# Going by halves of 256 tokens from one layer to the next in a two-block transformer kernel on one NeuronCore

## The chip, the cores and the metric

The kernel runs on one core of a Trainium2 chip (trn2). The metric is the device time of one execution in microseconds (us). Engines are named as the profile names them: PE is TensorE (PEld its weight loads), DVE is VectorE, ACT is ScalarE, POOL is GpSimd, SP is SyncE, which issues the weight transfers.

## The reference: what is computed

There are 512 tokens of 2048 features, in f32. The first block has one layer, the second has two. Cut to what matters here:

```python
# first block
u = rmsnorm(h, g_pre);  z = u @ w_in          # attention and a gated scan make y from z
h = h + rmsnorm(y @ w_out, g_post)            # new residual 1
gate = sigmoid(h @ w_pg);  e = p @ w_pp
h = h + rmsnorm(gate * e, g_ple)              # new residual 2
# second block, two layers
for l in range(2):
    z = rms_norm(h, pre_norm_g[l]) @ w_in[l]  # retention, differential attention and an LRU make y
    h = h + rms_norm(y @ w_out[l], post_norm_g[l])   # new residual 3 behind layer 0, the output behind layer 1
```

Each new residual is the input of the next matrix product at once: `w_pg` behind residual 1, the layer's `w_in` behind residuals 2 and 3.

## The kernel before, in words

**Tiling.** Features lie on the 128 partitions, tokens along the row, so an activation is 16 feature tiles of 128 x 512. A weight tile (128 output features) is 16 blocks of 128 x 128 and gives one output tile of 128 x 512 in one PSUM bank. A product of f32 precision is made of three fp32r matmuls: operand and weight are split into a high part (rounded to fp32r) and a low part (the rest), and PE adds high x high, high x low and low x high. An output tile is 48 matmuls of 512 columns, in four quarters of four blocks (`quarter`, L315 on). All weight tiles are numbered in one row (T_OUT: `w_out` of the first block, T_PG: `w_pg`, T_L2: the two layers).

**Who does what for the weights.** SP loads tile t into one of two raw buffers as soon as POOL has made the low parts of tile t-2 (L229). ACT makes the high part of a quarter (`high`, L710), once the raw tile has landed and PE has used this quarter of the tile before (`w_free`). POOL subtracts it from the raw tile (L262). `high_apart` (L717) and `low_parts_apart` (L270) do the same into a separate buffer, `next_weights`, which holds two whole tiles and lets them be converted ahead.

**Who does what for a new residual.** The last 16 tiles of a product go to PSUM banks; ACT squares each and copies it, times the gain, to `mixed` (L947, L722), DVE adds the squares up (L1633), and PE sums over the partitions with a matmul by ones, last `sum_rows_last` (L382 and L384, for the sum so far and for tile 15). ACT makes the inverse root with Ln and Exp (L729, L731) into a PSUM bank, `turned`. Then `new_operand` on DVE goes through the 16 tiles, four alone and then by pairs: `scale_tiles` (L1653, mixed times root), `add_tiles` (L1658, into the residual in `work`), and `low_tile` (L1616; L1618 with the next norm's gain) for the tiles one step behind. Between the add and the low tile ACT makes the high copy in `operand` (L916, L918). PE starts the next product with `three_tiles` (L341): three output tiles side by side in three banks, 9 matmuls per operand tile, so that PE follows the operand tile by tile; two of the weight tiles are those in `next_weights`, the third is in the usual place. PE takes operand tile k when `u_ready` says that its low part is there.

At residual 2 the 16 tiles are the gate: ACT makes Exp (L1112), DVE adds one, takes the reciprocal and multiplies by e (L1264, L1266, L1829), ACT squares (L1116) and copies with the gain.

**Behind residuals 2 and 3** the next norm's sum is taken while PE is at the first tiles: ACT issues four transfers of the residual to `out` (L1154), squares its 16 tiles (L1158), with conversions of weights between, DVE adds them up (L1631, L1633), and PE takes the ones matmul (L377) in the middle of the tile that follows the next one, at its second quarter. At residual 1 ACT issues four loads of e into `mixed` (L1103) between the high copies instead.

**Order.** Each engine's order is written out by hand in this file; there is no planner. An engine runs its instructions in order, so an instruction that waits holds back everything behind it on its engine. In `out_slots` ACT's order at the end is: tile 14, the eight conversions into `next_weights`, square and copy of tile 15, the high part of quarter 0 of the third weight tile, then Ln and Exp.

## Time and profile before

| | |
|---|---|
| Time, median of 3 runs | 3036.14 us (3035.97 to 3036.76) |
| The profiled execution's own time | 3036.43 us |
| Its span on the profile | 3034.6 us |
| PE busy | 2955.4 us (97%), 17162 matmuls |
| PEld busy | 2385.6 us (79%) |
| DVE busy | 1649.8 us (54%) |
| ACT busy | 1284.9 us (42%) |
| POOL busy | 1315.0 us (43%) |
| Mean granted clock of PE | 0.991 |

The times are what the device reports for an execution; the span runs from the first to the last profiled instruction; times in the rows are us from the span's start. A row of the page or of the grouped view ends with the busy time, the mean duration in ns and the idle time before, with what ended it. In the timeline a row has start and duration of an instruction, or of several like it that follow each other (x2); in square brackets stand the idle time of its engine before it and what ended that. Durations of matmuls overlap: what counts is how far apart they start.

### The profile page before, as it was taken

Reading aid. Unit: us, or ns where it says so; the run is one execution under the profiler, and the core shown is the slowest. Engines: PE = TensorE matmul, PEld = TensorE weight load, DVE = VectorE, ACT = ScalarE, POOL = GpSimd, SP = SyncE. Lnnn points to the kernel's source line nnn. Section 1 sums busy time; section 2 is a strip of 40 time slices with the busy share of each in tenths; the row PEclk is TensorE's granted clock in tenths of the full one; section 3 lists DMA queues with packets and bytes.
Section 4 is the critical chain, followed back from the end, with each engine's and each line's share of the span. In section 5 each row is a group of like instructions: output and inputs, shape, how many; then the busy total and the mean of one; then the engine's idle time right before and its main releaser. Section 6 shows DMA issues by size and latency. Waiting matters only on the chain.

```text
span 3034.6 us, 48369 instructions
## 1 busy us (share of the span) xinstructions
PE 2955.4 (97%) x17162; PEld 2385.6 (79%) x17162; DVE 1649.8 (54%) x2349; ACT 1284.9 (42%) x2468; POOL 1315.0 (43%) x1002
## 2 busy tenths in 40 slices
PE   8999999999999999989999999999999999999997
PEld 6888888877777787767887878788778878787886
DVE  5367666655656315657565664561275656654412
ACT  6545444354556333443333333453343333344432
POOL 4444444443433343553444444344444444444444
PEclk9999999999999999999999999999999999999999
DMA  6223222222222323233222222232242222222322
GB/s 238 102 90 111 83 83 76 77 84 83 78 77 80 125 97 139 90 118 125 105 87 91 87 85 82 83 142 100 104 156 88 95 87 96 84 84 80 143 97 97
DMA packets 60880, 305.72 MB, mean 101 GB/s; under 512 B 5712, under 2 KB 6096, under 8 KB 29776
## 3 DMA queue, kind: packets, MB, share of 16 engines
q1 hardware_dynamic: 38224, 259.54, 24.0%
q10 hardware_dynamic: 22528, 44.50, 4.2%
q8 instruction: 77, 1.26, 0.2%
q14 instruction: 51, 0.42, 0.0%
HBM read 285.67 MB, written 18.35 MB: 100 GB/s over the span
## 4 chain that ended last, share of the span: by engine, by line
issue 56%; POOL 32%; PE 9%; POOLq 1%; DMA 1%; ACT 1%; DVE 0%; DVEq 0%; ACTq 0%; SPq 0%
POOL w_low L262 31%; PE z L325 8%; DMA w_raw<-in_wt 1%; POOLq L261 1%; POOL next_weights L270 0%; PE scores L325 0%; PE v_bank L358 0%; PE z L358 0%; ACT u_high L722 0%; DVE mixed L1647 0%; POOLq L296 0%; DVE work L1266 0%; POOLq L284 0%; POOLq L129 0%; ACT w_high L710 0%
## 5 line engine op out<-in xcount | busy, mean ns | idle before, releaser
L262 POOL TENSOR_TENSOR w_low<-w_raw,w_high 128x512 fp32r<-128x512 f32 x932 | 1254.3, 1350 | 1700.0 <-ACT w_high L710 1692.5
L325 PE MATMUL z<-u_high,w_high 128*128 128x512 f32 x3408 | 1347.6, 395 | 2.6 <-POOL w_low L262 1.8
L325 PE MATMUL z<-u_high,w_low 128*128 128x512 f32 x3408 | 1328.4, 390 | 0.0
L325 PE MATMUL z<-u_low,w_high 128*128 128x512 f32 x3408 | 1327.0, 389 | 0.0
L710 ACT ACTIVATE w_high<-w_raw 128x512 fp32r<-128x512 f32 x928 | 578.7, 628 | 1223.0 <-PE z L325 1128.3
L325 PEld LDWEIGHTS z<-u_high,w_high 128*128 128x128 f32 x3408 | 640.1, 188 | 160.2 <-issue 23.3
L325 PEld LDWEIGHTS z<-u_high,w_low 128*128 128x128 f32 x3408 | 639.6, 188 | 136.1
L325 PEld LDWEIGHTS z<-u_low,w_high 128*128 128x128 f32 x3408 | 640.5, 188 | 127.1
L1633 DVE TENSOR_TENSOR work<-work 128x512 f32<-128x512 f32 x87 | 99.9, 1148 | 365.0 <-ACT work L947 351.7
L1260 DVE TENSOR_TENSOR work<-z,work 128x512 f32<-128x512 f32 x110 | 76.1, 692 | 122.7 <-PE z L325 101.8
L1292 DVE SCALAR_TENSOR_TENSOR work<-z,work 32x512 f32<-32x512 f32 (+1 forms) x176 | 120.9, 687 | 2.4
L735 ACT ACTIVATE work<-work 128x512 f32<-128x512 f32 x72 | 45.4, 631 | 145.4 <-DVE work L1272 92.1
L341 PE MATMUL z<-u_high,next_weights 128*128 128x512 f32 x192 | 72.1, 417 | 21.1 <-DVE u_low L1618 13.6
L722 ACT ACTIVATE values_spread<-work 32x512 f32<-32x512 f32 x128 | 80.6, 630 | 19.4 <-DVE work L1449 16.4
L1316 DVE TENSOR_TENSOR work<-o_bank,head_norm 128x512 f32<-128x512 f32 x28 | 19.4, 692 | 112.5 <-ACT head_norm L748 112.5
L1279 DVE TENSOR_TENSOR mixed<-work 128x512 f32<-128x512 f32 (+1 forms) x35 | 24.3, 694 | 85.4 <-ACT work L739 85.4
L1288 DVE SCALAR_TENSOR_TENSOR work<-z,work 128x512 f32<-128x512 f32 x56 | 38.7, 692 | 58.7 <-PE z L325 56.7
L1296 DVE TENSOR_TENSOR work<-work 128x512 f32<-128x512 f32 x56 | 65.4, 1168 | 5.2
L341 PEld LDWEIGHTS z<-u_high,next_weights 128*128 128x128 f32 x192 | 38.5, 200 | 35.5 <-issue 23.4
L1347 DVE TENSOR_TENSOR work<-work 128x512 f32<-128x512 f32 x56 | 55.0, 983 | 18.8 <-ACT work L722 10.8
L722 ACT ACTIVATE work<-work 128x512 f32<-128x512 f32 (+1 forms) x96 | 58.3, 639 | 13.9 <-DVE work L1347 9.7
L1474 DVE SCALAR_TENSOR_TENSOR work<-work 128x512 f32<-128x512 f32 x72 | 60.8, 845 | 6.0 <-issue 0.9
(281 smaller groups left out, 3243.7 us busy)
## 6 DMA issues: line engine op xcount, KB each, us to landing
w_raw<-in_wt SPq DMA_DIRECT2D x241, 1024.0 KB, 4.8
out_hT<-work ACTq DMA_DIRECT2D x8, 1024.0 KB, 8.7
work<-out_hT ACTq DMA_DIRECT2D x8, 1024.0 KB, 10.4
work<-in_xT SPq DMA_DIRECT2D x4, 1024.0 KB, 17.2
e_scratch<-work ACTq DMA_DIRECT2D x1, 4096.0 KB, 16.7
work<-in_xT ACTq DMA_DIRECT2D x4, 1024.0 KB, 10.9
work<-in_dec ACTq DMA_DIRECT2D x12, 256.0 KB, 2.7
work<-rope_tables ACTq DMA_DIRECT2D x10, 256.0 KB, 2.8
```

The source lines that it names most:

```text
L262: pool.tensor_tensor(WL[:, 4 * q:4 * q + 4, :], RAW[:, t.odd, 512 * q:512 * q + 512].rearrange("p (k c) -> p k c", k=4), WH[:, 4 * q:4 * q ...
L325: mm = pe.matmul(bank[:], w[:, k, :], u[:, k, :], start=(k == 0 and n == 0), stop=(k == KT - 1 and n == 2))
L341: mm = pe.matmul(bank[:], w[x], u[:, k, :], start=(k == 0 and n == 0), stop=(k == KT - 1 and n == 2))
L710: act.activation(WH[:, 4 * q:4 * q + 4, :], RAW[:, n.odd, 512 * q:512 * q + 512].rearrange("p (k c) -> p k c", k=4), ACT.Copy).then_inc(se ...
L722: i = act.activation(dst, src, ACT.Copy, **kw)
L735: act.activation(row(r), row(r), ACT.Exp, scale=-1.0)
L1260: v.tensor_tensor(dst, (Z[t.odd] if bank is None else bank)[:], row(RSTD), ALU.mult).then_inc(sem("z_free"), 1)
L1292: i = v.scalar_tensor_tensor(out=row(TM)[o:o + half], in0=z[x:x + half, :], scalar=-scale if first else scale, in1=row(sin)[o:o + half], o ...
L1296: v.tensor_tensor(row(dst), row(dst), row(TM), ALU.add)
L1347: i = v.tensor_tensor(x, x, y, ALU.mult)
L1474: v.scalar_tensor_tensor(out=R_, in0=R_, scalar=-1.0 / f, in1=TB, op0=ALU.add, op1=ALU.mult)
L1633: i = v.tensor_tensor(row(ACC), row(ACC), row(SQ0 + s), ALU.add)
```

## The change

At the three new residuals (behind `w_out` of the first block, behind `w_pg`, behind `w_out` of layer 0) everything from the last output tile to the three opening tiles goes in two halves of 256 tokens:

- PE: tile 15 is `split_tile`: all 48 matmuls for tokens 0 to 255 into one bank, then all 48 for tokens 256 to 511 into another, each with 256 columns. The ones matmuls are two halves too: `sum_first_half` within the second half of tile 15 (behind its first quarter, at residual 2 behind its third), `sum_second_half` within the first half of the opening tiles (behind operand tile 1, at residual 2 behind tile 4). `three_tiles` goes through the 16 operand tiles twice, 144 matmuls of 256 columns each time. Quarters of weights are given back in the second pass only.
- ACT: square and copy of tile 15, Ln and Exp by halves (`root_half`, in a bank for each half). `operand` makes 16 high copies of 128 x 256, then 16 more. The three other conversions of the third weight tile stand behind the copies 0, 3 and 5 of the first half at all three residuals (before: at residuals 1 and 3 among the copies, at residual 2 ahead of the root). What tile 15's second half needs of ACT stands among the copies too.
- DVE: `new_operand` runs twice, tile 0 and 1 alone and then seven pairs, with 256 elements of each tile; at residual 2 the second half's gate stands behind its third step.

The rest of the kernel, the four loads of e, the four transfers to `out` and the chain of squares are as before; the loads of e stand behind the copies 7, 11, 13 and 15 of the second half.

The diff, cut (PE, then ACT, then DVE):

```diff
@@ -214,6 +214,8 @@
             return (XW if buf is None else buf)[:, r, :].rearrange("p (k c) -> p k c", k=4)
         PH, PL = UL[:, 12:14, :], UL[:, 14:16, :]
         ROOT = TP[1]
+        SPLIT_BANK, SUM_BANK, ROOTS = [TP[0], VB], SC[1], [TP[1], SC[1]]
+        HALVES = [slice(0, S // 2), slice(S // 2, S)]
         OUT_BANK = SC[0]
         FIRST = {1: [Z[0], Z[1]], 2: [Z[0], VB]}
         LAST = [SC[0], SC[1], TP[0], OB, Z[0], Z[1]]
...
-                    mm.then_inc(sem("w_free"), 3)
+            def three_tiles(t, gen, g, n, at):
+
+                pe.wait_ge(sem("z_free"), t.times(1, -T_HGG - 1))
+                for half, cols in enumerate(HALVES):
+                    for q in range(4):
+                        if half == 0:
+                            pe.wait_ge(sem("l_ready"), t.times(4, 8 + q + 1))
+                        for k in range(4 * q, 4 * q + 4):
+                            if half == 0:
+                                pe.wait_ge(sem("u_half"), g * 16 + k + 1)
+                            else:
+                                pe.wait_ge(sem("u_ready"), gen * 16 + k + 1)
+                            c = slice((k - 4 * q) * P, (k - 4 * q + 1) * P)
+                            hi = [XW[:, r + q, c] for r in XHI] + [WH[:, k, :]]
+                            lo = [XW[:, r + q, c] for r in XLO] + [WL[:, k, :]]
+                            for x, bank in enumerate((Z[0], Z[1], SC[0])):
+                                for i, (w, u) in enumerate(((hi, UH), (hi, UL), (lo, UH))):
+                                    mm = pe.matmul(bank[:, cols], w[x], u[:, k, cols], start=(k == 0 and i == 0),
+                                                   stop=(k == KT - 1 and i == 2))
+                            if half == 0 and k == at:
+                                sum_second_half(n)
+                        if half == 1:
+                            mm.then_inc(sem("w_free"), 3)
+
+            def split_tile(t, n, g, at):
+
+                pe.wait_ge(sem("z_free"), t.times(1, -1 - T_HGG))
+                for half, cols in enumerate(HALVES):
+                    for q in range(4):
+                        if half == 0:
+                            pe.wait_ge(sem("l_ready"), t.times(4, q + 1))
+                        for k in range(4 * q, 4 * q + 4):
+                            for i, (w, u) in enumerate(((WH, UH), (WH, UL), (WL, UH))):
+                                mm = pe.matmul(SPLIT_BANK[half][:, cols], w[:, k, :], u[:, k, cols], start=(k == 0 and i == 0),
+                                               stop=(k == KT - 1 and i == 2))
+                        if half == 1:
+                            mm.then_inc(sem("w_free"), 1)
+                            if q == at:
+                                sum_first_half(n, g)
+                    if half == 0:
+                        mm.then_inc(sem("z_half"), 1)
+
+            def sum_first_half(n, g):
+
+                c = HALVES[0]
+                pe.wait_ge(sem("sq_used"), PRIMED + n + 15)
+                pe.matmul(SUM_BANK[:, c], ONES[:], row(ACC)[:, c], start=True, stop=False)
+                pe.wait_ge(sem("sq_half"), g + 1)
+                pe.matmul(SUM_BANK[:, c], ONES[:], row(SQ1)[:, c], start=False, stop=True).then_inc(sem("sum_half"), 1)
+
+            def sum_second_half(n):
+
+                c = HALVES[1]
+                pe.matmul(OB[:, c], ONES[:], row(ACC)[:, c], start=True, stop=False)
+                pe.wait_ge(sem("sq_ready"), n + 16)
+                pe.matmul(OB[:, c], ONES[:], row(SQ1)[:, c], start=False, stop=True).then_inc(sem("sq_used"), 1)
 
             def pair_step(t, k, gen, block=1):
 
...
-            three_tiles(Tile(T_PG), 2)
+            for q in range(4):
+                quarter(Tile(T_OUT + 14), q)
+            split_tile(Tile(T_OUT + 15), 16, 0, 0)
+            three_tiles(Tile(T_PG), 2, 0, 16, 1)
             for m in range(3, 6):
...
                 for s in range(2):
                     for q in range(4):
                         quarter(Tile(T_PG + s, (2, i)), q)
-            sum_rows_last(32)
+            for q in range(4):
+                quarter(Tile(T_PG + 14), q)
+            split_tile(Tile(T_PG + 15), 32, 1, 2)
 
             for l in range(LAYERS):
-                three_tiles(Tile(T_L2 + l * PER_LAYER), l * 2 + 3)
+                three_tiles(Tile(T_L2 + l * PER_LAYER), l * 2 + 3, l + 1, 64 if l else 32, 1 if l else 4)
                 for m in range(3, LRU_TILES):
                     for q in range(4):
                         quarter(Tile(T_L2 + R_LX + m, (PER_LAYER, l)), q, None, LX_BANK[m])
...
+            def root_half(half, wait, done):
+
+                c = HALVES[half]
+                act.wait_ge(*wait)
+                act.activation(row(ACC)[:, c], (OB if half else SUM_BANK)[:, c], ACT.Ln, bias=CS[:, C_EPS:C_EPS + 1], scale=1.0 / D)
+                act.drain()
+                act.activation(ROOTS[half][:, c], row(ACC)[:, c], ACT.Exp, scale=-0.5).then_inc(sem(done), 1)
+
+            def operand(t, g, new, second, scale=None, done=None):
+
+
+
+                n = t.times(4)
+                steps = {0: lambda: high(t.plus(1), 1, n - 2), 3: lambda: high(t.plus(1), 2, n - 1), 5: lambda: high(t.plus(1), 3, n)}
+                for half, cols in enumerate(HALVES):
+                    for m in range(KT):
+                        if half:
+                            act.wait_ge(sem("h_new"), m + 1 + new)
+                        else:
+                            act.wait_ge(sem("h_half"), g * 16 + m + 1)
+                        act.activation(UH[:, m, cols], W[:, H + m, cols], ACT.Copy,
+                                       scale=1.0 if scale is None else scale[:, m:m + 1]).then_inc(sem("uh_ready" if half else "uh_half"), 1)
+                        if half == 0 and m in steps:
+                            steps[m]()
+                        if half == 0 and m in second:
+                            second[m]()
+                        if half and m in (7, 11, 13, 15):
+                            q = (7, 11, 13, 15).index(m)
+                            if done is not None:
+                                done(q, *((0, 8), (8, 12), (12, 14), (14, 16))[q])
+                            if q < 3:
+                                high(t.plus(2), q, n + 3 + 3 * q)
...
                             high_apart(t.plus(16 + x), q, x)
-                one(t.plus(15), 15, 1, n + 14, quarters=0)
                 if last == "three":
+                    a = HALVES[0]
+                    act.wait_ge(sem("z_half"), split + 1)
+                    act.wait_ge(sem("sq_used"), PRIMED + n + 14)
+                    act.activation(row(SQ1)[:, a], SPLIT_BANK[0][:, a], ACT.Square).then_inc(sem("sq_half"), 1)
+                    copy(MIX[:, 15, a], SPLIT_BANK[0][:, a], scale=gain[:, 15:16])
                     high(t.plus(17), 0, t.times(4, 61))
-                inv_root(OB, row(ACC), D, (sem("sq_used"), PRIMED + n + 16), root, ROOT[:])
+                    root_half(0, (sem("sum_half"), split + 1), "root_half")
+                else:
+                    one(t.plus(15), 15, 1, n + 14, quarters=0)
+                    inv_root(OB, row(ACC), D, (sem("sq_used"), PRIMED + n + 16), root, ROOT[:])
...
@@ -1139,16 +1213,36 @@
             pg_square(14, 0, 15)
             for q in range(4):
                 high_apart(Tile(T_L2 + 1), q, 1)
-            pg_evict(Tile(T_PG + 15), 1, 32 + 14)
-            for q in range(4):
-                high(Tile(T_L2 + 1), q, 4 * T_L2 - 3 + q)
-            pg_square(15, 1, 16)
-            inv_root(OB, row(ACC), D, (sem("sq_used"), PRIMED + 48), "root_ready", ROOT[:])
+            def pg_evict_half(half, wait, done):
+
+                c = HALVES[half]
+                act.wait_ge(*wait)
+                act.activation(row(SQ1)[:, c], SPLIT_BANK[half][:, c], ACT.Exp, scale=-1.0).then_inc(sem(done), 1)
+
+            def pg_square_half(half, wait, done):
+
+                c = HALVES[half]
+                act.wait_ge(*wait)
+                act.activation(row(SQ1)[:, c], MIX[:, 15, c], ACT.Square).then_inc(sem(done), 1)
+                act.drain()
+                copy(MIX[:, 15, c], MIX[:, 15, c], scale=PR1[:, G_PLE + 15:G_PLE + 16])
+
+            act.wait_ge(sem("sq_used"), PRIMED + 32 + 14)
+            pg_evict_half(0, (sem("z_half"), 2), "ze_half")
+            high(Tile(T_L2 + 1), 0, 4 * T_L2 - 3)
+            pg_square_half(0, (sem("pg_half"), 1), "sq_half")
+            root_half(0, (sem("sum_half"), 2), "root_half")
 
             for l in range(LAYERS):
                 three = 4 * (T_L2 + l * PER_LAYER)
-                operand(Tile(T_L2, (PER_LAYER, l)), W[:, H:H + 16, :], PR2[:, l, G2_PRE:G2_PRE + 16], l * 16 + 16,
-                        weights=False, taken=three + 3, third=three if l else None)
+                if l:
+                    second = {2: lambda: out_second(Tile(T_L2 + R_OUT), 64, PR2[:, 0, G2_POST:G2_POST + 16]),
+                              4: lambda: root_half(1, (sem("sq_used"), PRIMED + 80), "root_ready")}
+                else:
+                    second = {1: lambda: pg_evict_half(1, (sem("w_free"), 4 * T_L2), "z_free"),
+                              4: lambda: pg_square_half(1, (sem("pg_prod"), 16), "sq_ready"),
+                              6: lambda: root_half(1, (sem("sq_used"), PRIMED + 48), "root_ready")}
+                operand(Tile(T_L2 + l * PER_LAYER), l + 1, l * 16 + 16, second, PR2[:, l, G2_PRE:G2_PRE + 16])
                 act.wait_ge(sem("h_new"), l * 16 + 32)
                 for g in range(4):
                     act.dma_start(out[4 * g:4 * g + 4].rearrange("m p t -> p m t"), W[:, H + 4 * g:H + 4 * g + 4, :]
...
@@ -1658,20 +1752,44 @@
                 v.tensor_tensor(W[:, H + m:H + m + k, :], W[:, H + m:H + m + k, :], MIX[:, m:m + k, :],
                                 ALU.add).then_inc(sem("h_new"), k)
 
-            def new_operand(root, n, loaded, scale=None):
-
-                wait_apart("root_ready", root)
+            def new_operand(root, n, g, loaded, scale=None, between={}):
+
+                wait_apart("root_half", g + 1)
                 v.wait_ge(sem("x0_loaded"), 16)
                 v.wait_ge(sem("h_loaded"), loaded)
-                lows = 0
-                for m, k in ((0, 1), (1, 1), (2, 1), (3, 1), (4, 2), (6, 2), (8, 2), (10, 2), (12, 2), (14, 2)):
-                    scale_tiles(m, k)
-                    add_tiles(m, k)
-                    while lows < m:
-                        low_tile(lows, n, W[:, H:H + 16, :], scale)
-                        lows += 1
-                for m in range(lows, 16):
-                    low_tile(m, n, W[:, H:H + 16, :], scale)
+                for half, cols in enumerate(HALVES):
+                    if half:
+                        wait_apart("root_ready", root)
+                    lows = 0
+                    for m, k in ((0, 1), (1, 1), (2, 2), (4, 2), (6, 2), (8, 2), (10, 2), (12, 2), (14, 2)):
+                        b = ROOTS[half][:, cols]
+                        b = bass.AP(b.tensor, b.offset, [b.ap[0], [0, k], [1, S // 2]])
+                        v.tensor_tensor(MIX[:, m:m + k, cols], MIX[:, m:m + k, cols], b, ALU.mult)
+                        v.drain()
+                        x = W[:, H + m:H + m + k, cols]
+                        v.tensor_tensor(x, x, MIX[:, m:m + k, cols], ALU.add).then_inc(sem("h_new" if half else "h_half"), k)
+                        while lows < m:
+                            low_half(lows, n, g, half, scale)
+                            lows += 1
+                        if half == 0 and m in between:
+                            between[m]()
+                    for m in range(lows, KT):
+                        low_half(m, n, g, half, scale)
...
@@ -1850,10 +1968,22 @@
                         pg_sum(s, i * 2 + 32 + s + 1)
             pg_tile(14, 0, T_PG + 13)
             pg_sum(0, 47)
-            pg_tile(15, 1, T_PG + 14)
+            def pg_last_half(half, wait, done):
+
+                c = HALVES[half]
+                v.wait_ge(*wait)
+                s = row(SQ1)[:, c]
+                v.tensor_scalar(s, s, 1.0, None, ALU.add)
+                v.drain()
+                v.reciprocal(s, s)
+                v.drain()
+                v.tensor_tensor(MIX[:, 15, c], s, MIX[:, 15, c], ALU.mult).then_inc(sem(done), 1)
+
+            pg_last_half(0, (sem("ze_half"), 1), "pg_half")
 
             for l in range(LAYERS):
-                new_operand(l + 2, l * 32 + 48, l * 64 + 64, PR2[:, l, G2_PRE:G2_PRE + 16])
+                new_operand(l + 2, l * 32 + 48, l + 1, l * 64 + 64, PR2[:, l, G2_PRE:G2_PRE + 16],
+                            {} if l else {2: lambda: pg_last_half(1, (sem("z_free"), T_PG + 16 - T_HGG), "pg_prod")})
 
                 sum_squares(l * 32 + 48)
                 wait_apart("rstd_ready", l + 2)
```

## Rows read from the trace of the kernel before

A line of "..." stands for rows left out.

**Rows 1.** Page, part 1: busy time, share of the span and instructions.

```profile
PE 2955.4 (97%) x17162; PEld 2385.6 (79%) x17162; DVE 1649.8 (54%) x2349; ACT 1284.9 (42%) x2468; POOL 1315.0 (43%) x1002
```

**Rows 2.** Waits of PE: waiting line, releaser: us in total, times, longest.

```profile
PE z L341 <- DVE u_low L1618: 13.6, 5, 5.6
PE o_bank L377 <- DVE work L1633: 1.6, 2, 0.8
```

**Rows 3.** Timeline of PE, residual 1.

```profile
1160.78 1.02 PE L382 MATMUL o_bank<-work,ones 128*128 128x512 f32 x2
...
1168.43 0.77 PE L341 MATMUL z<-u_high,next_weights 128*128 128x512 f32 x1 [5.68 <-DVE u_low L1616]
...
1205.88 0.39 PE L341 MATMUL scores<-u_high,w_low 128*128 128x512 f32 x1
1206.11 0.39 PE L325 MATMUL scores<-u_high,w_high 128*128 128x512 f32 x1
```

**Rows 4.** Windows, residual 1: stretch, then PE, PEld, DVE, ACT, POOL busy, clock.

```profile
1168.40:1173.60 5.20, 5.17 (x12) 4.13 (x13) 5.05 (x7) 1.83 (x4) 1.75 (x1) 0.50 0.00 0
```

**Rows 5.** Timeline of ACT, residual 1.

```profile
1157.14 2.19 ACT L717 ACTIVATE next_weights<-w_raw 128x512 fp32r<-128x512 f32 x4 [3.21 <-DMA w_raw<-in_wt]
...
1162.90 0.63 ACT L710 ACTIVATE w_high<-w_raw 128x512 fp32r<-128x512 f32 x1 [0.75 <-DMA w_raw<-in_wt]
```

**Rows 6.** Timeline of POOL, residual 1.

```profile
1152.45 5.15 POOL L270 TENSOR_TENSOR next_weights<-w_raw,next_weights 128x512 fp32r<-128x512 f32 x4 [0.29 <-ACT next_weights L717]
...
1169.05 1.75 POOL L262 TENSOR_TENSOR w_low<-w_raw,w_high 128x512 fp32r<-128x512 f32 x1 [4.18 <-ACT w_high L710]
```

**Rows 7.** Timeline of DVE, residual 1.

```profile
1164.87 0.69 DVE L1653 TENSOR_TENSOR mixed<-mixed,turned 128x512 f32<-128x512 f32 x1 [12.16 <-ACT turned L731]
...
1169.57 1.78 DVE L1616 TENSOR_TENSOR u_low<-work,u_high 128x512 fp32r<-128x512 f32 x1
...
1173.23 1.21 DVE L1653 TENSOR_TENSOR mixed<-mixed,turned 128x1024 f32<-128x1024 f32 x1
1174.52 1.23 DVE L1658 TENSOR_TENSOR work<-work,mixed 128x1024 f32<-128x1024 f32 x1
...
1179.40 1.28 DVE L1616 TENSOR_TENSOR u_low<-work,u_high 128x512 fp32r<-128x512 f32 x2
...
1199.39 1.96 DVE L1616 TENSOR_TENSOR u_low<-work,u_high 128x512 fp32r<-128x512 f32 x2 [1.47 <-ACT u_high L916]
```

**Rows 8.** Timeline of DVE, residual 2.

```profile
1352.09 3.35 DVE L1266 RECIPROCAL work<-work 128x512 f32<-128x512 f32 x1
...
1361.62 0.69 DVE L1653 TENSOR_TENSOR mixed<-mixed,turned 128x512 f32<-128x512 f32 x1 [4.27 <-ACT turned L731]
...
1379.45 1.41 DVE L1618 SCALAR_TENSOR_TENSOR u_low<-work,params,u_high 128x512 fp32r<-128x512 f32 x2
```

**Rows 9.** Timeline of ACT, residual 2.

```profile
1347.28 2.18 ACT L717 ACTIVATE next_weights<-w_raw 128x512 fp32r<-128x512 f32 x4
...
1394.20 0.71 ACT L918 ACTIVATE u_high<-work,params  x1
...
1397.54 1.76 ACT L1158 ACTIVATE work<-work 128x512 f32<-128x512 f32 x3 [2.63 <-issue]
...
1401.20 0.63 ACT L710 ACTIVATE w_high<-w_raw 128x512 fp32r<-128x512 f32 x1 [1.11 <-PE scores L341]
```

**Rows 10.** Timeline of PE at the ones matmul, residual 2.

```profile
1418.22 1.12 PE L377 MATMUL o_bank<-work,ones 128*128 128x512 f32 x2 [0.80 <-DVE work L1633]
```

**Rows 11.** The same, residual 3.

```profile
2247.51 1.13 PE L377 MATMUL o_bank<-work,ones 128*128 128x512 f32 x2 [0.81 <-DVE work L1633]
```

**Rows 12.** Timeline of PE, 128-column matmuls, and the page's weight loads.

```profile
1601.68 0.39 PE L533 MATMUL o_bank<-work 128*128 128x128 f32 x2
1601.91 0.39 PE L535 MATMUL o_bank<-work 128*128 128x128 f32 x2
...
L325 PEld LDWEIGHTS z<-u_high,w_high 128*128 128x128 f32 x3408 | 640.1, 188 | 160.2 <-issue 23.3
```

82 lines of the change are left out of this document (35 added, 47 removed).

## The prediction

> **What bounds the kernel now.** I read the page first: PE is busy for 97% of the span and DVE for 54% [rows 1], so only time in which PE stands can come back. The waits of PE, longest in total first, say where [rows 2]: at L341, the three opening tiles, PE waits for `u_low` of DVE (L1618 at the second and third residual; L1616 at the first is alike), and twice 0.8 us at L377, the ones matmul over the squares of the new residual. The timeline at the first new residual [rows 3]: tile 15 ends at 1160.78, two pairs of ones matmuls follow, and the first opening matmul starts at 1168.43 after 5.68 us of idle; the next tile starts at 1206.11. Matmuls start 0.2265 us apart, so the 144 of this stage need 32.6 us, and the stretch has 45.3. The windows show what follows the idle: 12 matmuls in 5.2 us at granted clock 0.50 (1.2 GHz, 0.427 us each) [rows 4]. The third residual is alike. The second is longer, because the sigmoid runs before its norm: a reciprocal alone is 3.35 us [rows 8].
>
> But the stage has a second limit. After the idle DVE works nearly without a gap from 1164.87 to 1201.35, 36.5 us [rows 7], against 32.6 of PE. **DVE is within a few us of being the bound of exactly these stages.** And the end of a second or third residual is set later still: ACT squares the residual, DVE adds, and PE stands 0.8 us at L377 until the last add is done [rows 2, 10, 11].
>
> **The change, part by part.** I call the residuals R1, R2, R3.
>
> *PE's own work.* Per residual 48 + 144 matmuls of 512 columns become 384 of 256. None of this size with changing weights is in the trace. From below, half of 0.2265 is 0.113. The f32 matmuls of L533 and L535 with 128 columns, each behind a weight load of its own, start 0.11 us apart (two in 0.23) [rows 12], so a load fits into that. From above stands the 0.188 us that a load is busy [rows 12]. I take 0.1165, near the first, since the row that overlaps loads is the nearest. An opening stage is then 288 x 0.1165 + 0.9 for the second half's ones matmuls = 34.5 us.
>
> *Start of the first half, R1.* Half A of tile 15 ends at 1160.78 - 5.4 = 1155.3. ACT is then in its queue at the four conversions of 1157.14, done at 1159.33; behind them square, copy, and the conversion of w_high of 1162.90, which waits for the weight transfer [rows 5]. That transfer can't be earlier: it needs the buffer that POOL gives back at 1152.45 + 5.15 = 1157.6 [rows 6], and nothing there moves. Ln and Exp stand behind this conversion, as before. So the square can be early, the root can't. Shorter Ln and Exp bring 0.5 us, of which POOL's conversion of 1163.6, now in DVE's way, takes a little: DVE starts 0.4 earlier, not 5. PE meanwhile waits inside tile 15 for the square (from 1157.2 to 1159.8, 2.6 us), ends at 1164.4, and gets its first operand near 1166.9 instead of 1168.43. R3 has the same rows and order, 0.4.
>
> *Start, R2.* ACT is free at 1347.28 + 2.18 = 1349.46 [rows 9]. Exp of half 0.4, plus one on DVE beside POOL 1.1, reciprocal 1.7 (half of 3.35) with its drains 0.2, product 0.7, square 0.5, ones matmul 0.6, Ln and Exp 0.9: 1355.5, where DVE began at 1361.62 [rows 8]: 6.1 earlier.
>
> *DVE's length, the main term.* From the rows [rows 7]: an add behind its scale starts 0.08 after the scale's end, so 0.76 apart at 512 elements and 1.29 at 1024, or 1.035 ns an element; an instruction without a drain starts 0.08 before the last one ends, so an add takes 0.61 or 1.14 and a low tile 0.60 (two in 1.28). With 256 elements: scale 0.49, add 0.345, low 0.34. Before: 4 x (0.76 + 0.61) + 6 x (1.29 + 1.14) + 16 x 0.60 = 29.7. After, in each half: 2 x (0.49 + 0.345) + 7 x (0.76 + 0.61) + 16 x 0.34 = 16.7, twice 33.4: **3.7 more**. R2 and R3 use the scaled low tile, 0.66 (two in 1.41) [rows 8] and 0.395 in half: 30.6 becomes 35.2, 4.6 more. Together 12.9 us. What DVE took above the 29.7 in R1, 6.8, I keep: 1.47 is a wait for ACT, and six conversions of POOL stop it for 0.9 each (1.78 instead of 0.68 while POOL runs 1.75) [rows 6, 7]; the same six lie in the new stage. The ends for an instruction of 256: half of a whole one (12.9 falls to 0), and the whole fixed part exposed each time (below). I take the extrapolation, since 512 and 1024 lie on one line.
>
> The Trainium skill, VectorE: DVE Perf Modes, the section on the errata, says that a small tile pays a fixed latency of its own, about 151 cycles at 0.96 GHz for a tensor_tensor of f32, and advises tiles of 512 elements or more: a rule against this change. There are 32 more instructions per residual (68 for 36); at 0.157 us each that would be an estimate of 5.0 per residual, 15 in all instead of 12.9, and a time near 3043.6. The rows show part of this cost overlapped.
>
> *R1, the sum.* DVE ends at 1201.35 + 3.7 - 0.4 = 1204.65. The last two low tiles come 0.34 apart and PE needs 1.05 for each: PE ends 1.9 later, 1206.5. Before, 1206.11 [rows 3]: **+0.4**. By PE alone it would be 1166.9 + 34.5 = 1201.4, so 5 us of PE slack hide its waits, its pace, and a lower clock if that comes.
>
> *R2.* DVE's end: -6.1 + 4.6, + 2.6 for the gate of the second half, which the change puts into DVE's queue behind the third tile (0.3 + 1.7 + 0.4 and drains; it ran in the idle before), + 2.7 for three conversions of the third tile's weights, which fell in the idle and now fall in DVE's loop (3 x 0.9) = +3.8. Then the squares: ACT starts them when the last high copy and four output transfers are issued (first square 1397.54) [rows 9]. The last copy (1394.20 to 1394.91) came 1.3 before DVE's end, since two whole low tiles followed; now it comes 0.3 before: +1.0. The chain of squares then waited 1.11 us for PE to leave the stage [rows 9], and about as long once more for the next tile's first quarter; coming later, it no longer waits: -2.3. PE at L377 starts at 1418.22 + 2.5: **+2.5** [rows 10]. PE reaches that point 72 matmuls, 16.3 us, after its stage's end and stands there.
>
> *R3.* -0.4 + 4.6 + 1.0 - 2.3 = **+2.9** on 2247.51 [rows 11].
>
> Sum +5.8. Smaller: in R1 the transfers of `e` are issued some 14 us later, in half B, and land near 1206, just before the gate wants them at 1208; I count nothing (0 to 2). The old low clock costs little to lose: DVE had the last word. I round down to +5 for conversions that share one wait. The profiled execution took 3036.43, the median is 3036.14: forecast **3041**.
>
> **The rivals.**
> *DVE keeps ahead (faster).* For it: the idle of 5.68 us at R1 is real [rows 3], and PE starts 1.5 to 8 earlier. Against: the 36.5 us of DVE. If a half instruction cost half a whole one, 12.9 goes: 3028. If PE alone set the end, R1 gives -4.8, R3 -5, R2 1357.8 + 34.5 against 1418.22 - 0.8 - 16.3 = 1401.1, -8.8: 3017.
> *The weight load bounds the matmul (slower).* At 0.188 an opening stage is 55 us; R1 would end at 1223.8, +17.7, three times +53: 3089. It decides from 0.134 on, where 288 matmuls use up the 5 us of slack. Against: the 0.111 [rows 12].
> *ACT holds the high copies back (slower).* In half A the second half's square, copy, Ln, Exp and three conversions stand among the 16 high copies; Ln waits for PE's ones matmul, and DVE's low tiles wait behind. Price 2 to 3 us at each residual: 3048. It decides once the wait at Ln passes the 1.4 us that a scale and add give.
> *Nothing moves:* the halves cancel and DVE's end stays, 3036.
>
> **How the numbers follow.** A measurement here can tell about 0.2%, 6 us, from no change: same is 3030.1 to 3042.2. Forecast 0.55 (its own range 3034 to 3047, 0.35 of it within 0.2%, 0.20 slower), DVE ahead 0.19 (0.18 faster), ACT 0.14, weight load 0.05, nothing 0.07. Faster 0.18, same 0.43, slower 0.39. The range leaves out the weight load and the far side of the first rival: 3027 to 3051.
>
> **What would show it.** Right: DVE from first scale to last low tile 40 us in R1 instead of 36.5, 256-element instructions at 0.42, the root of half A at R1 starting near 1163.5 behind the conversion, PE idle in many pieces before `u_low` at the opening matmuls, and a longer wait at L377's ones matmul. Wrong: opening matmuls back to back (DVE ahead), starts 0.19 apart (load), or DVE waiting for `u_high` (ACT). The forecast falls if the root of half A comes before 1160, or if no wait at the sum of squares grows.

## The result, and the profile after

The changed kernel takes **3046.77 us** (median of 7 runs, 3044.88 to 3049.72), beside 3036.26 for the kernel before: ratio 1.0034, 95% interval 1.0023 to 1.0045, or 10.5 us slower. Its executions lie within 4.8 us of each other, those of before within 2.0. The profiled execution took 3046.97 us, its span is 3045.2 us and the granted clock 0.991. Half A is tokens 0 to 255, half B the rest.

The page's busy line [rows 1] and the waits of PE [rows 2] (waiting line, releaser, us in total, times, longest):

```profile
PE 2969.9 (98%) x17750; PEld 2423.9 (80%) x17750; DVE 1660.0 (55%) x2448; ACT 1295.6 (43%) x2529; POOL 1314.8 (43%) x1002
```

```profile
PE z L348 <- DVE u_low L1791: 9.8, 11, 2.2
...
PE o_bank L420 <- DVE work L1727: 6.5, 2, 4.0
...
PE scores L379 <- ACT work L1226: 4.0, 1, 4.0
PE scores L379 <- ACT work L1028: 3.9, 2, 2.0
...
PE z L348 <- DVE u_low L1789: 2.1, 4, 0.7
```

L348 is the opening stage (L341 before): its waits fell from 21.1 us (13.6 behind L1618, 7.5 behind L1616), in pieces of up to 5.7, to 11.9 in fifteen smaller ones. L379 is new: the wait inside tile 15. **L420 is the ones matmul over the squares (L377 before), and its waits rose from 1.6 to 6.5.**

R1 in the timelines of ACT, DVE and PE [rows 3, 5, 7]:

```profile
1156.93 2.19 ACT L771 ACTIVATE next_weights<-w_raw 128x512 fp32r<-128x512 f32 x4 [3.24 <-DMA w_raw<-in_wt]
1159.03 0.36 ACT L1028 ACTIVATE work<-turned 128x256 f32<-128x256 f32 x1
1159.29 0.46 ACT L776 ACTIVATE mixed<-turned,params 128x256 f32<-128x256 f32 x1
1162.65 0.63 ACT L764 ACTIVATE w_high<-w_raw 128x512 fp32r<-128x512 f32 x1 [2.90 <-DMA w_raw<-in_wt]
1163.19 0.46 ACT L960 ACTIVATE work<-scores,constants 128x256 f32<-128x256 f32 x1
```

```profile
1164.19 0.42 DVE L1767 TENSOR_TENSOR mixed<-mixed,turned 128x256 f32<-128x256 f32 x1 [11.72 <-ACT turned L962]
...
1201.15 1.64 DVE L1789 TENSOR_TENSOR u_low<-work,u_high 128x256 fp32r<-128x256 f32 x2 [1.17 <-ACT u_high L976]
```

```profile
1166.42 0.36 PE L348 MATMUL z<-u_high,next_weights 128*128 128x256 f32 x1 [0.48 <-DVE u_low L1789]
...
1204.66 0.28 PE L348 MATMUL scores<-u_high,w_low 128*128 128x256 f32 x1
1204.78 0.40 PE L327 MATMUL scores<-u_high,w_high 128*128 128x512 f32 x1
```

The root of half A (L960) stands behind the conversion that waits 2.90 us for the weights. DVE works 38.6 us, from 1164.19 to 1202.79, where it took 36.5. Matmuls of 256 columns start 0.12 us apart. The next tile begins 1.3 us earlier than before.

Now the ends of R2 and R3: ACT's first squares [rows 9], PE at the ones matmul [rows 10, 11], and windows of 3.4 us behind it (stretch, busy time of PE, PEld, DVE, ACT, POOL, then the granted clock):

```profile
1399.58 1.76 ACT L1252 ACTIVATE work<-work 128x512 f32<-128x512 f32 x3 [2.25 <-issue]
```

```profile
1416.62 0.39 PE L327 MATMUL turned<-u_high,w_low 128*128 128x512 f32 x1
1420.97 2.08 PE L420 MATMUL o_bank<-work,ones 128*128 128x512 f32 x2 [3.97 <-DVE work L1727]
...
2256.01 1.22 PE L420 MATMUL o_bank<-work,ones 128*128 128x512 f32 x1 [2.52 <-DVE work L1727]
```

```profile
1420.97:1424.40 3.43, 3.43 (x6) 2.11 (x7) 0.00 (x0) 0.26 (x1) 2.31 (x2) 0.50 0.90 289
1424.40:1427.80 3.40, 3.40 (x12) 2.66 (x12) 0.00 (x0) 0.20 (x1) 0.00 (x0) 0.68 0.29 118
...
2256.00:2259.40 3.40, 3.39 (x6) 2.08 (x7) 0.00 (x0) 0.00 (x0) 2.30 (x2) 0.50 0.93 298
2259.40:2262.80 3.40, 3.40 (x16) 2.79 (x16) 0.00 (x0) 1.19 (x2) 0.48 (x1) 1.00 0.26 108
```

In the kernel before, where PE stood only 0.8 us, the same stretch has 13 matmuls at full clock:

```profile
1418.22:1421.60 3.38, 3.38 (x13) 2.46 (x14) 0.00 (x0) 0.00 (x0) 2.33 (x2) 1.00 0.91 311
```

So PE stands 4.0 and 2.5 us, and **then runs at 1.2 GHz for a while**: a cost that no term of the forecast held.

The wait at R2 is 1.4 us longer than at R3, and ACT's squares do not explain it. From the first square to the ones matmul it takes 21.4 us at R2 and 20.0 at R3. DVE's adds are the same, but its idle time between them, for which the profile shows no releaser ("issue"), is 5.3 us in all at R2 and 3.7 at R3 (timeline of DVE, two rows of R2, then two of R3):

```profile
1408.25 0.69 DVE L1727 TENSOR_TENSOR work<-work 128x512 f32<-128x512 f32 x1 [0.57 <-issue]
1409.21 0.69 DVE L1727 TENSOR_TENSOR work<-work 128x512 f32<-128x512 f32 x1 [0.27 <-issue]
...
2243.60 0.69 DVE L1727 TENSOR_TENSOR work<-work 128x512 f32<-128x512 f32 x1 [0.45 <-issue]
2244.45 0.69 DVE L1727 TENSOR_TENSOR work<-work 128x512 f32<-128x512 f32 x1 [0.16 <-issue]
```

In the traces of the runs below the long gaps stand at R2 whenever DVE's instructions are those of the change (five more traces), and the short ones in the two that split R2 and edit DVE's instructions (more work for DVE, groups of four): there PE stands 2.5 us at R2 too. R3 always has the short ones. Why is not shown.

Counted from the start of tile 15 of each residual (1149.91, 1339.11, 2173.59 before; 1149.66, 1337.78, 2179.07 after):

| us from tile 15's start | before | after | difference |
|---|---|---|---|
| R1, next tile | 56.2 | 55.1 | -1.1 |
| R2, next tile / ones matmul | 61.8 / 79.1 | 62.7 / 83.2 | +0.9 / +4.1 |
| R2's ones matmul to R3's tile 15 | 755.4 | 758.1 | +2.7 |
| R3, next tile / ones matmul | 56.6 / 73.9 | 57.9 / 76.9 | +1.3 / +3.0 |
| R3's ones matmul to the end | 787.1 | 789.2 | +2.1 |

With the 0.25 by which R1's tile 15 starts earlier this is 10.6, the difference of the spans. In the third and fifth row the code is as before, and what differs is above all the clock behind the ones matmul. It is 0.50 for some 5.6 us at R2 and 3.4 at R3, and half of such a stretch is lost: 2.8 and 1.7 us. The other 0.4 of the fifth row is less than what traces at full clock differ by there (over 1 us).

### The profile page after: what moved, and what is told of

It reads as the page before. It is cut to its first block, busy times and chain, and to the rows that moved or that the text cites. A ratio compares the mean times of both kernels' runs of the same rounds, so it can differ in the third digit from the quotient of the medians.

```text
span 3045.2 us, 49473 instructions
## 1 busy us (share of the span) xinstructions
PE 2969.9 (98%) x17750; PEld 2423.9 (80%) x17750; DVE 1660.0 (55%) x2448; ACT 1295.6 (43%) x2529; POOL 1314.8 (43%) x1002
## 4 chain that ended last, share of the span: by engine, by line
issue 56%; POOL 32%; PE 9%; POOLq 1%; DMA 1%; ACT 1%; DVE 0%; DVEq 0%; ACTq 0%; SPq 0%
POOL w_low L264 31%; PE z L327 8%; DMA w_raw<-in_wt 1%; POOLq L263 1%; POOL next_weights L272 0%; PE scores L327 0%; PE v_bank L401 0%; PE z L401 0%; ACT u_high L776 0%; DVE mixed L1741 0%; POOLq L298 0%; DVE work L1360 0%; POOLq L286 0%; POOLq L129 0%; ACT w_high L764 0%
## 5 line engine op out<-in xcount | busy, mean ns | idle before, releaser
L327 PE MATMUL z<-u_high,w_high 128*128 128x512 f32 x3360 | 1329.2, 396 | 2.5 <-POOL w_low L264 1.8
L327 PE MATMUL z<-u_high,w_low 128*128 128x512 f32 x3360 | 1310.0, 390 | 0.0
L327 PE MATMUL z<-u_low,w_high 128*128 128x512 f32 x3360 | 1308.5, 389 | 0.0
L764 ACT ACTIVATE w_high<-w_raw 128x512 fp32r<-128x512 f32 x928 | 579.0, 628 | 1223.8 <-PE z L327 1127.4
L327 PEld LDWEIGHTS z<-u_high,w_high 128*128 128x128 f32 x3360 | 631.0, 188 | 157.8 <-issue 23.3
L327 PEld LDWEIGHTS z<-u_high,w_low 128*128 128x128 f32 x3360 | 630.6, 188 | 134.4
L327 PEld LDWEIGHTS z<-u_low,w_high 128*128 128x128 f32 x3360 | 631.4, 188 | 125.9
L348 PE MATMUL z<-u_high,next_weights 128*128 128x256 f32 x384 | 89.4, 295 | 12.0 <-DVE u_low L1791 9.8
L348 PEld LDWEIGHTS z<-u_high,next_weights 128*128 128x128 f32 x384 | 67.8, 195 | 16.2 <-DVE u_low L1791 8.8
```

The source lines that it names most:

```text
L327: mm = pe.matmul(bank[:], w[:, k, :], u[:, k, :], start=(k == 0 and n == 0), stop=(k == KT - 1 and n == 2))
L348: mm = pe.matmul(bank[:, cols], w[x], u[:, k, cols], start=(k == 0 and i == 0), stop=(k == KT - 1 and i == 2))
L764: act.activation(WH[:, 4 * q:4 * q + 4, :], RAW[:, n.odd, 512 * q:512 * q + 512].rearrange("p (k c) -> p k c", k=4), ACT.Copy).then_inc(se ...
```

## The experiments

Each was timed in five rounds beside the kernel before (medians 3036.2 to 3036.3). "The change" is the changed kernel; a median stands with its number of runs and the ratio's interval.

### Where the loss lies: the ones matmul

**The ones matmul later, in the change.** ACT's root over it moves as far.

```
-                        if m == 4 and q == 1:
+                        if m == 4 and q == 3:
                             sum_rows(row(ACC), OB, (sem("sq_used"), PRIMED + l * 32 + 64), "ss_done")
...
-                        if m == 4 and q == 2:
+                        if m == 5 and q == 0:
                             inv_root(OB, row(RSTD), D, (sem("ss_done"), l + 2), "rstd_ready")
```

> The changed kernel with the ones matmul over the squares of the new residual (R2 and R3) two quarters of a tile later in PE's order (5.4 us of matmuls), and ACT's root behind it two quarters later too. Theory (DVE and the chain of squares are late by 3 to 4 us, PE stands for them at this one matmul, 4.14 and 2.69 us, and runs behind it at half the clock for 6.8 and 3.4 us of records, some 5.1 us lost): both waits and both low clocks go, 6.8 + 5.1 = 11.9 us, 3035. Rival A (the wait is only the place where a late stage shows; banks and root are then late downstream): PE stands elsewhere before the first retention tile, 3044 to 3047. Rival B (the extra time lies in the opening stages, in the narrow matmuls): no change at all, 3047, with the two waits gone from the trace all the same.

Measured 3036.45 (11 runs, 0.9991 to 1.0009): 10.3 of the 10.5 us are back. PE no longer stands there (timeline of PE):

```profile
1425.16 1.02 PE L420 MATMUL o_bank<-work,ones 128*128 128x512 f32 x2
```

Both rivals fall: the wait comes back nowhere, and the opening stages, untouched, were not where most of the time went.

**The same move in the kernel before.**

> The kernel before with the same move of the ones matmul and of the root. Theory: only its two waits of 0.8 us are there to win and no clock falls behind them: 3034.5, same within 0.1%. If the move itself costs something downstream (root 5.4 us later), it shows here undisturbed: 3038 or more.

Measured 3034.52 (11 runs, 0.9986 to 1.0004), 1.7 below its neighbour, as expected: the two waits of 0.8, and no cost of the move, though the interval does not exclude a difference of nothing. So the 10.3 is not a gain that any kernel would have had: 8.6 of it belong to the change. With the wait out of the way in both, the halves are still 1.9 us slower (3036.45 against 3034.52); the intervals overlap, so it isn't shown that these are more than noise.

**The ones matmul earlier, in the kernel before** (q == 0, ACT's root at q == 1). Nothing is split here.

> The kernel before with the ones matmul one quarter (2.72 us) earlier, so that PE stands 3.5 us at it at R2 and at R3, as in the changed kernel, with nothing split. Theory: 5.4 us of waits, and behind each the granted clock falls for 3.4 to 6.8 us of records (1.7 to 3.4 lost): 3045 to 3048, nearly the whole loss of the change. Rival C (the low clock of the changed kernel comes from its many small idle pieces in the opening stage, not from this wait): clock stays at full, 3041.6. Rival A (downstream slack absorbs a wait here): 3036 to 3038.

Measured 3045.71 (7 runs, 1.0019 to 1.0041), +9.5. Timeline and windows:

```profile
1419.10 1.63 PE L377 MATMUL o_bank<-work,ones 128*128 128x512 f32 x2 [3.49 <-DVE work L1633]
```

```profile
1419.60:1423.00 3.40, 3.40 (x8) 2.35 (x7) 0.00 (x0) 0.00 (x0) 0.57 (x1) 0.50 0.90 335
1423.00:1427.00 4.00, 4.00 (x19) 3.25 (x18) 0.23 (x1) 1.84 (x3) 1.30 (x1) 1.00 0.07 23
...
2253.00:2256.40 3.40, 3.40 (x8) 1.99 (x8) 0.00 (x0) 0.00 (x0) 0.60 (x1) 0.58 0.93 337
```

Waits of 3.5 us were made by hand twice, 5.4 us more than before, and the clock fell behind both. Counted to the next tile 15 and to the end, less the quarter that now stands behind the ones matmul, the low clock costs 1.4 and 1.6 us. About 1 of the 9.3 by which this trace's span is longer lies ahead of R1, where nothing is changed. So two waits alone make some 8.4 us, most of the loss of the change, without any of its halves.

### Which residual carries it

**R2 put back to whole tiles** (its `split_tile`, `three_tiles`, `operand`, `new_operand` replaced by those of before).

> The changed kernel with R2 (the second residual) put back to whole tiles, R1 and R3 by halves. Theory: R2 carries 4.1 us of later ones matmul and 3.4 us of low clock: 3039 to 3040, no low clock behind its ones matmul. If R3 carried the loss: 3045.

Measured 3038.62 (11 runs, 0.9998 to 1.0016). PE stands 0.8 us at R2's ones matmul, as before the change; at R3 it stands 2.5, and in this trace the clock stays full behind it.

**R2 and R3 put back**, only R1 by halves.

> The changed kernel with R2 and R3 put back to whole tiles, only R1 by halves. Theory: R1 alone moves its next tile 1.1 us earlier against its own start, there is no ones matmul behind it, and nothing else differs: 3035.0, same as before within 0.1%; then R3 carries the difference to the run with only R2 whole (3038.6), 3.6 us. Rival (the narrow matmuls or the late transfers of e cost at R1 too): 3037 to 3038.

Measured 3034.85 (11 runs, 0.9986 to 1.0004). The steps against the kernel before (3036.31) are R1 -1.5, R3 +3.8, R2 +8.2: in sum 10.5. R2 is the costly one, as expected. R1's -1.5 is not clear of noise: its interval includes no change, and in its trace R1's next tile comes 56.4 us after the start of tile 15, where it was 56.2.

### What makes the chain late

**More work for DVE** in half B.

```
+                        if half:
+                            v.tensor_tensor(MIX[:, m, cols], MIX[:, m, cols], MIX[:, m, cols], ALU.max)
+                            v.drain()
                         v.tensor_tensor(MIX[:, m:m + k, cols], MIX[:, m:m + k, cols], b, ALU.mult)
```

> The changed kernel with one more DVE instruction of 256 elements (0.42 us and a drain, 0.5 in all, its result unused) ahead of each of the nine scales of half B, at R1, R2 and R3. Theory (DVE sets the end of the stage and of the chain of squares): the last low tile comes 4.5 us later each time, the next tile too, the wait at the ones matmul stays as it is since both shift: 3 x 4.5 = 13.5, 3060. Rival (PE with its narrow matmuls, or ACT, sets the end and DVE has room): 3047 to 3050.

Measured 3053.57 (5 runs, 1.0043 to 1.0070): +6.8, half of the 13.5. Each added instruction does take 0.50 us of DVE (timeline):

```profile
1184.37 0.42 DVE L1768 TENSOR_TENSOR mixed<-mixed 128x256 f32<-128x256 f32 x1
1184.87 0.69 DVE L1770 TENSOR_TENSOR mixed<-mixed,scores 128x512 f32<-128x512 f32 x1
```

DVE's stage grew by 3.1 us in R1, 5.9 in R2 and 2.1 in R3 instead of 4.5 each. In R1 its last wait for `u_high` shrank from 1.17 to 0.66, and POOL's conversions fell on other instructions; in R2 a wait of 3.0 for `u_high` came on top. PE's next point (the next tile of R1, the ones matmuls of R2 and R3) came 9 us later in all. I had also expected the waits at the ones matmul to stay. R2's fell from 3.97 to 2.56, with the short gaps of DVE described above, and PE went on at full clock, which returned 2.6 us. So the missing 6.7 us are in part an added instruction that shows only half to two thirds at R1 and R3, in part that clock. DVE's length sets the end; the rival (room on DVE) is out.

**Groups of four**, 12 DVE instructions fewer.

```
-                    for m, k in ((0, 1), (1, 1), (2, 2), (4, 2), (6, 2), (8, 2), (10, 2), (12, 2), (14, 2)):
+                    for m, k in ((0, 1), (1, 1), (2, 2), (4, 4), (8, 4), (12, 4)):
```

> The changed kernel with DVE's scales and adds of the later tiles in groups of four (1024 elements) instead of two: 12 instructions fewer per residual, the elements the same. Theory (DVE's fixed part per instruction is what the halves cost): 12 x 0.08 us (the part that stays visible between instructions without a drain) is 1 us per residual, up to 1.9 if the whole fixed part counts; the wait at the ones matmul falls from 4.1 and 2.7 to about 3.2 and 1.8, 3044, and 3042 if the low clock of R3 goes with it. Rival (ACT and PE wait for the coarser groups: the first tile of a group comes 0.5 to 0.7 us later): 3047 or slower, with more DVE waits for u_high.

Measured 3046.54 (5 runs, 1.0022 to 1.0050): no gain, near the rival's number. DVE's waits for `u_high` went from 4.9 us in all to 14.1; the longest is in R2 (timelines of ACT and DVE):

```profile
1373.40 0.47 ACT L960 ACTIVATE work<-o_bank,constants 128x256 f32<-128x256 f32 x1 [4.44 <-PE o_bank L386]
```

```profile
1374.80 0.48 DVE L1791 SCALAR_TENSOR_TENSOR u_low<-work,params,u_high 128x256 fp32r<-128x256 f32 x1 [3.16 <-ACT u_high L976]
```

ACT stands at the Ln of half B for PE's ones matmuls, and DVE behind it. In the change's own trace the same row waits 2.15 us:

```profile
1367.95 0.47 ACT L960 ACTIVATE work<-o_bank,constants 128x256 f32<-128x256 f32 x1 [2.15 <-PE o_bank L386]
```

The difference is how long PE runs at half clock in R2's opening: one window of the run with groups of four, then one of the change.

```profile
1366.00:1369.00 3.00, 2.34 (x11) 2.34 (x12) 2.93 (x5) 2.64 (x6) 0.35 (x1) 0.50 0.00 0
```

```profile
1366.00:1369.00 3.00, 3.00 (x23) 2.80 (x23) 2.75 (x4) 0.98 (x3) 0.78 (x1) 1.00 0.32 68
```

The total hides a gain elsewhere: in this trace the ones matmul of R2 waits 2.55 us and PE goes on at full clock, so that 2.5 us less are lost behind it, while R1's next tile comes 1.9 later and R2's ones matmul 0.8.

**The root of half B later on ACT**, here at R3; at R1 it is 4 and at R2 6 that become 10.

```
-                              4: lambda: root_half(1, (sem("sq_used"), PRIMED + 80), "root_ready")}
+                              10: lambda: root_half(1, (sem("sq_used"), PRIMED + 80), "root_ready")}
```

> The changed kernel with ACT's Ln and Exp of half B behind the eleventh high copy of half A instead of the fifth (R1, R3) or seventh (R2). Theory (the slower rival of the prediction is at work beside the main cause: Ln waits for PE's pair of ones matmuls, 2.1 us in the profile, up to 4.4 where PE's low clock of R2 lasts longer, and DVE's low tiles wait behind): DVE's waits for u_high of 1.1 to 2.8 us go, the executions spread less, 3044 to 3045. Rival (DVE's own work covers it): 3047 and the same spread.

Measured 3044.29 (8 runs, 1.0016 to 1.0037), 2.5 below the change, and the runs lie within 2.6 us instead of 4.8. In R2 ACT no longer waits at it:

```profile
1371.33 0.45 ACT L960 ACTIVATE work<-o_bank,constants 128x256 f32<-128x256 f32 x1
```

The forecast's third rival is real, and worth at most some 2.5 us in all: the intervals of the two overlap, and 1.2 us of it in the trace is a shorter stretch of low clock behind R2's ones matmul, where PE stood 3.98 us as in the change.

**The output transfers later**: the four issues leave the front of the squares and stand behind the squares of tiles 8, 10, 12 and 14.

> The changed kernel with the four output transfers of R2 and R3 issued on ACT among the last squares instead of ahead of the first. Theory (ACT's queue, 2.6 us of issues behind the last u_high copy, delays the chain of squares): the first square comes 1 to 2 us earlier, right behind the last low tile; the waits at the ones matmul fall to 2.5 and 1, the low clock of R3 and perhaps of R2 goes: 3038 to 3042. Rival (DVE's last low tile releases the chain anyway, and issues among the squares stretch it): 3046 to 3048.

Measured 3039.14 (11 runs, 1.0001 to 1.0019), 7.6 below the change. ACT squares right behind its last copy, DVE's adds begin where its last low tile ends (1.7 us behind it in the change), PE's waits fall to 1.29 and 0.80, and the clock stays (timelines of ACT and PE, window):

```profile
1399.91 0.89 ACT L976 ACTIVATE u_high<-work,params 128x256 fp32r<-128x256 f32 x2
1400.71 1.14 ACT L1249 ACTIVATE work<-work 128x512 f32<-128x512 f32 x2
```

```profile
1421.79 1.13 PE L420 MATMUL o_bank<-work,ones 128*128 128x512 f32 x2 [1.29 <-DVE work L1728]
...
2250.54 0.70 PE L420 MATMUL o_bank<-work,ones 128*128 128x512 f32 x1 [0.80 <-DVE work L1728]
```

```profile
1421.79:1425.20 3.41, 3.41 (x13) 2.53 (x14) 0.00 (x0) 1.09 (x2) 2.53 (x2) 1.00 1.03 336
```

### What held the split back at its start

**The root of half A ahead of the waiting conversion** (R1, R3).

```
-                    high(t.plus(17), 0, t.times(4, 61))
                     root_half(0, (sem("sum_half"), split + 1), "root_half")
+                    high(t.plus(17), 0, t.times(4, 61))
```

> The changed kernel with ACT's Ln and Exp of half A ahead of the conversion of w_high that waits 2.9 us for a weight transfer, at R1 and R3. Theory (that conversion holds the root, so the split of tile 15 brings nothing there): DVE starts 2.5 to 2.8 us earlier at R1 and R3 and ends as much earlier, the next tile of R1 comes 2 earlier, the wait at R3's ones matmul shrinks from 2.7 to below 1 and its low clock (1.7) goes: 3041. Rival (PE then stands for w_low of the same tile, and DVE for u_high): 3045 to 3047.

Measured 3043.57 (6 runs, 1.0018 to 1.0042), 3.2 below the change; 3041 was expected. The six lie 9.6 us apart (3041.77 to 3051.34), so the 3.2 is not clear of noise. The root starts 2.6 us earlier, and so does DVE:

```profile
1160.58 0.47 ACT L960 ACTIVATE work<-scores,constants 128x256 f32<-128x256 f32 x1 [0.91 <-PE scores L379]
...
1161.91 0.63 ACT L764 ACTIVATE w_high<-w_raw 128x512 fp32r<-128x512 f32 x1 [0.40 <-DMA w_raw<-in_wt]
```

```profile
1161.60 0.42 DVE L1767 TENSOR_TENSOR mixed<-mixed,turned 128x256 f32<-128x256 f32 x1 [9.48 <-ACT turned L962]
```

But DVE's loop in R1 is 1.7 longer: POOL's conversions now meet its first low tile (1.52 us instead of 0.42) and two of its four small adds, which take 647 ns on average instead of 426 (groups of DVE in R1's stretch, this run, then the run with R2 whole, whose R1 is as in the change).

```profile
L1770 DVE TENSOR_TENSOR work<-work,mixed 128x256 f32<-128x256 f32 x4 | 2.6, 647 | 0.3
```

```profile
L1832 DVE TENSOR_TENSOR work<-work,mixed 128x256 f32<-128x256 f32 x4 | 1.7, 426 | 0.3
```

I had also expected R3's wait at the ones matmul to shrink, and its low clock to go with it. The wait could not: PE's arrival and the chain of squares move together with DVE's end, and it is 2.55. The clock stayed full behind it all the same, which is 1.6 us of the gain of this trace. That can't be put down to the edit: behind the same wait the clock fell in the change.

### Put together

**Late ones matmul, early root of half A, late root of half B**; then the same with R2 whole.

> The changed kernel with three things put together: the ones matmul two quarters later, the root of half A ahead of the conversion that waits for the weights (R1, R3), the root of half B behind the eleventh high copy. Theory: from 3036.5 with the first alone, -3.2 for the second and about -2 for the third: 3031.3, 0.16% below the kernel before. If the gains overlap: 3033 to 3036.

> As the run before, with R2 put back to whole tiles. Theory: 3038.6 with R2 whole, less 3.3 at the ones matmuls, less 3.2 for the earlier roots of half A, less up to 1 for the root of half B: 3031 to 3032. If R2 by halves is now worth something (with the root of half B out of the way), this one is the slower of the two by 1 to 2 us.

Measured 3034.36 (11 runs, 0.9985 to 1.0003) and 3034.11 (11 runs, 0.9986 to 1.0004): the gains overlap, as the second half of the first expectation had it; the second missed its 3031 to 3032. Whether R2 goes by halves or whole makes no difference (0.25 us). In the trace of the first the earlier root lets DVE start 2.9 us earlier at R1 by tile 15's start, but its loop takes 41.7 us instead of 38.6, and PE's next tile comes no earlier. With these orders the split costs nothing, but neither run can be told from the kernel before, nor from the kernel before with the late ones matmul (3034.52). No version here is shown to beat it.

## Why the prediction was right or wrong

The forecast, 3041 with slower at 0.39 beside same at 0.43, put "same" slightly ahead, and slower by over 0.2% is what came. The measured 3046.77 lies in the range (to 3051), 5.8 above the forecast. That is in part luck: the range reached so far up for the rival of ACT (3048), and the largest part of the miss is a cost that the forecast had nowhere. Differences below are counted from the start of tile 15.

- **What bounds the kernel: right.** DVE was the second limit behind PE's idle. PE was given its operand 2 us earlier at R1 and 7 at R2, and the stages still ended where DVE ended. The first rival (DVE keeps ahead) is excluded by its own sign: PE waits in fifteen pieces.
- **PE's own work: right.** Matmuls of 256 columns start 0.12 apart (0.1165 taken), weight loads of 195 ns hidden beside them. The rival at 0.188 is out. (By the terms it gives, 1166.9 + 55, it would have ended R1 at 1221.9 rather than 1223.8.)
- **Start, R1 and R3: right.** The root came at 1163.19 (forecast near 1163.5), behind the conversion; the earlier root in the experiment shows that nothing else held it for the last 2.6 us.
- **Start, R2: right within 1 us.** 1354.70 with tile 15 starting 1.3 earlier than before, so 1356.0 on the forecast's clock; forecast 1355.5.
- **DVE's length, the main term: right in kind, too large in R1.** 38.6 us against 40, because three of POOL's conversions meet an add of half A and cost 0.35 each, not 0.9; the three that meet low tiles of half B cost 0.9 to 1.1. At R2 it took 43.9 (44.5 by the forecast's terms) and at R3 41.6 (41.7). By the Trainium skill, VectorE: DVE Perf Modes, the section on the errata, each of many small tiles pays its fixed latency. The rows bear that out in part only: instructions of 256 elements take 0.42 and start 0.34 apart in a row, and nine added ones of 0.50 lengthened the loops of R1 and R3 by 3.1 and 2.1. The estimate that went with it, 3043.6 (3043.1 if 2.1 is added to the forecast's 3041), came nearer to the result, but DVE's stages were no longer than the forecast's own terms; the loss behind them brought it there.
- **R1, the sum +0.4: measured -1.1.** That shorter loop: what POOL's conversions cost DVE was taken over from before at its old price. The late loads of `e` cost nothing, as counted: they are issued 1.2 to 8.8 us later, not 14, and DVE never waits for them.
- **R2, the sum +2.5: measured +4.1.** DVE's end came 3.7 later, forecast 3.8. Two terms behind it failed, in opposite directions.
  - **"Coming later, it no longer waits: -2.3" was mis-sized.** The chain's two waits for PE (1.11 and 1.04) did go, but from the first square to the ones matmul it took 21.4 us where it had taken 20.7, +0.7. DVE's adds and the gaps between them set its pace, not ACT; 1.4 us of it are the longer gaps. With the short ones it would have been -0.7, still not -2.3.
  - **"Now it comes 0.3 before: +1.0" was wrong.** The last high copy ended at 1397.33, 1.25 before DVE's end where it had been 1.35, since both last low tiles still follow it. The first square came 3.4 later, where 4.8 was forecast.
- **R3, the sum +2.9: measured +3.0, but by luck.** DVE's end came 4.0 later (4.2), the first square 3.6 (5.2), and the chain took 0.6 less (2.3 less): the same two errors, which cancel here.
- **The missing term: the clock behind the longer wait, 4.8 us in the table, some 4.5 of it by the low stretches.** The forecast wrote that slack hides "a lower clock if that comes", and looked for it only in the opening stage. Behind the ones matmul PE has no slack. The parts add up: -0.25 and -1.1 at R1, +4.1, +2.7, +3.0 and +2.1 are the 10.6.
- **The third rival (ACT holds the high copies back) was not exclusive.** It acts beside the main cause; its price, 2 to 3 per residual, is at most 2.5 for all three.

What stays open: why the low clock in R2's opening lasts longer in some traces. It does so in kernels whose code is the same up to there (DVE's stage of R2 takes 43.9 us in the change, 46.2 with the late output transfers), and the spread shrinks once ACT's Ln no longer depends on PE's progress; I did not vary it by itself. Open too is what makes DVE's gaps between the adds of R2 long or short.

## What to carry to other kernels

Before splitting work to start the next stage earlier, find what sets that stage's end: an engine that works without a gap through it gets only more instructions from the split. Price a wait of PE outside the stages with slack as the wait plus what the clock may lose behind it, and look there first for a remedy: moving one matmul by 5.4 us of its own queue brought the time 10.3 of 10.5 us down (1.7 of them it gives without the change too), where four remedies ahead of it brought between 0.2 and 7.6. And compare traces wait by wait before a gain is put down to an edit: of the same wait of 2.5 us, some traces pay 1.7 us more than others. An instruction that waits for PE (a root) in the middle of copies that PE itself needs belongs behind them.

## What the runs showed of the hardware

- The clock behind a short wait of PE. At the ones matmul over the squares, in the traces of all kernels here: behind waits of 0.8 to 1.3 us PE went on at full clock (seven of seven), behind 3.5 to 4.0 us at 1.2 GHz (five of five), and behind 2.5 to 2.6 us at 1.2 GHz four times and at full clock four times. Inside tile 15 (L379 in the change) waits of 1.8 to 2.3 us at R1 and R3 were followed by 1.2 GHz in 12 of 21 cases. In the change it is so at R1: behind 1.99 us the matmuls of 256 columns start 0.21 apart for 3 us. At the ones matmul the low clock cost 1.4 to 2.7 us a time, 0.4 to 0.8 of the wait. In the run with R2 whole the 2.5 us of R3 were followed by full clock:

```profile
2247.97:2251.40 3.43, 3.43 (x13) 2.51 (x14) 0.00 (x0) 0.00 (x0) 2.32 (x2) 1.00 0.97 344
```

- POOL's cost to DVE depends on which instruction it meets. In R1 of the changed kernel a conversion stretched an add of 512 elements from 0.69 to 1.06 us, and two low tiles from 0.75 to 1.85 (timeline of DVE). Half of what the earlier root of half A brought at R1 and R3 was paid back so.

```profile
1166.94 1.06 DVE L1770 TENSOR_TENSOR work<-work,mixed 128x512 f32<-128x512 f32 x1
...
1190.33 0.69 DVE L1770 TENSOR_TENSOR work<-work,mixed 128x512 f32<-128x512 f32 x1
1190.94 1.85 DVE L1789 TENSOR_TENSOR u_low<-work,u_high 128x256 fp32r<-128x256 f32 x2
...
1194.07 0.75 DVE L1789 TENSOR_TENSOR u_low<-work,u_high 128x256 fp32r<-128x256 f32 x2
```
